# The first expert group's token gather, cut into two halves of 256 columns

## The reference, cut to what matters

```
def moe_ffn(x, router_w, router_bias, w_gate, w_up, w_down):
    aff = sigmoid(x @ router_w)                       # 16 experts, 4 groups of 4
    # the group with the best two-score sum, and its two best experts, per token
    comb = one_hot(e_idx) * gate / sum(gate)          # weight of each token in each expert
    hg = einsum('btd,edf->btef', x, w_gate)           # 2048 -> 512
    hu = einsum('btd,edf->btef', x, w_up)
    h  = silu(hg) * hu * comb[..., None]
    return einsum('btef,efd->btd', h, w_down)         # 512 -> 2048
```

## Time and profile before

| | us |
|---|---|
| median of three runs | 1759.06 |
| the profiled execution's own time | 1759.79 |
| its span in the trace | 1757.9 |
| PE busy | 1596.2 (91%) |
| DVE busy | 720.8 (41%) |
| ACT busy | 467.4 (27%) |

### The profile page before, as it was taken

One profiled execution on the slowest core, in us unless ns is written; L12 is line 12 of the kernel. 1 busy time (PEld: TensorE's weight loads), 2 busy tenths in 40 slices (PEclk: granted clock), 3 DMA queues, 4 the chain that ended last, 5 costly groups with the idle time before them and its releaser, 6 DMA issues.

```text
span 1757.9 us, 18363 instructions
## 1 busy us (share of the span) xinstructions
PE 1596.2 (91%) x7223; PEld 948.4 (54%) x7223; DVE 720.8 (41%) x1220; ACT 467.4 (27%) x693; POOL 16.8 (1%) x36
## 2 busy tenths in 40 slices
PE   8999999998999879898879999999799988989985
PEld 6888887876533224333237888878543323533321
DVE  6675555656211112111157797656521112111116
ACT  4565545432110001000024335553220000100000
POOL 1000000000000000000000000000000000000000
PEclk9999999998999999999999999999899999999998
DMA  8666554784899999999994555538489999999995
GB/s 267 174 180 182 166 158 141 262 310 157 319 416 421 421 416 422 419 422 421 421 361 120 168 167 162 162 121 347 175 354 421 421 421 416 421 415 422 421 419 234
DMA packets 133270, 538.12 MB, mean 306 GB/s; under 512 B 19377, under 2 KB 19505, under 8 KB 86849
## 3 DMA queue, kind: packets, MB, share of 16 engines
q1 hardware_dynamic: 132608, 532.75, 80.0%
q0 software_dynamic: 576, 4.19, 0.6%
HBM read 534.82 MB, written 2.10 MB: 305 GB/s over the span
## 4 chain that ended last, share of the span: by engine, by line
PE 56%; issue 29%; DMA 10%; DVE 3%; ACT 1%; SPq 1%; POOL 0%; POOLq 0%; DVEq 0%; ACTq 0%
PE ps L750 12%; PE ps L752 11%; PE ps L751 11%; PE ps L1035 8%; DMA ring<-in_moe_w_down 5%; PE ps L1097 4%; DMA ring<-in_moe_w_up 4%; PE ps L731 2%; PE ps L1015 1%; PE ps L1016 1%; PE ps L1024 1%; PE ps L1208 1%; PE ps L1222 1%; DMA arena<-in_x 0%; SPq L597 0%
## 5 line engine op out<-in xcount | busy, mean ns | idle before, releaser
L750 PE MATMUL ps<-w_lo,x_hi 128*128 128x512 f32 x880 | 350.7, 399 | 7.5 <-DVE x_lo L2312 2.5
L751 PE MATMUL ps<-w_hi,x_hi 128*128 128x512 f32 x880 | 344.7, 392 | 0.0
L1768 DVE TENSOR_TENSOR w_lo<-ring,w_hi 128x1024 fp32r<-128x1024 f32 x224 | 270.2, 1223 | 181.2 <-ACT w_hi L1315 179.6
L1315 ACT ACTIVATE w_hi<-ring 128x1024 fp32r<-128x1024 f32 x224 | 235.5, 1059 | 311.5 <-PE ps L752 306.8
L2210 DVE TENSOR_TENSOR arena<-ps,arena 128x512 f32<-128x512 f32 x128 | 82.9, 687 | 418.7 <-PE ps L1025 418.7
L750 PEld LDWEIGHTS ps<-w_lo,x_hi 128*128 128x128 f32 x880 | 166.5, 189 | 46.3 <-issue 7.2
L1035 PE MATMUL ps<-arena,hT 128*64 128x512 f32 x768 | 177.1, 616 | 9.6 <-DVE hT L2200 4.3
L751 PEld LDWEIGHTS ps<-w_hi,x_hi 128*128 128x128 f32 x880 | 166.5, 189 | 34.7 <-issue 0.5
L1097 PE MATMUL ps<-ring,arena 128*64 128x512 f32 x768 | 170.5, 594 | 6.4 <-DMA ring<-in_moe_w_down 6.4
L1524 ACT ACTIVATE y_hi<-ps 128x512 fp32r<-128x512 f32 x64 | 36.1, 596 | 459.9 <-PE ps L1097 239.7
L752 PE MATMUL ps<-w_hi,h_lo 128*128 128x512 f32 x384 | 150.2, 391 | 0.0
(11 more groups left out here) (333 smaller groups left out, 1530.8 us busy)
## 6 DMA issues: line engine op xcount, KB each, us to landing
arena<-in_moe_w_gate SPq DMA_DIRECT2D x48, 2048.0 KB, 18.3
ring<-in_moe_w_down SPq DMA_DIRECT2D x96, 1024.0 KB, 18.2
arena<-in_moe_w_up SPq DMA_DIRECT2D x32, 2048.0 KB, 20.4
ring<-in_moe_w_up SPq DMA_DIRECT2D x32, 2048.0 KB, 20.7
ring<-in_ab_w_in SPq DMA_DIRECT2D x96, 512.0 KB, 3.7
ring<-in_moe_w_gate SPq DMA_DIRECT2D x16, 2048.0 KB, 19.9
arena<-in_moe_w_down SPq DMA_DIRECT2D x32, 1024.0 KB, 17.1
ring<-in_c_w_in SPq DMA_DIRECT2D x64, 512.0 KB, 3.7
```

What stands on the lines that cost most here:

```text
L750: nc.tensor.matmul(t, x_h, w_l[:, k, :], start=(opens and k == 0), stop=False)
L751: nc.tensor.matmul(t, x_h, w_h[:, k, :], start=False, stop=False)
L1315: act.activation(high_unit(n), raw_unit(n)[0], ACT.Copy).then_inc(w_hi_ready, 1)
L1768: v.tensor_tensor(lo, raw, high_unit(n).bitcast(FP32), ALU.subtract).then_inc(w_lo_ready, 1)
```

## The change

In the first group, a gather tile is made in two parts. `gather_tile` makes only the first 256 columns (`HALF_GROUP`; the slots of pairs 0 and 1), and the copies are of 256 columns. The other 256 columns (pairs 2 and 3) are made by `gather_rest`: tiles 0 to 7 behind the first pair's last projection step and ahead of the turning of `h_e`, tiles 8 to 15 two by two ahead of each m of the second pair. The first picks are written by halves: the first 256 columns of both blocks where the picks were, the second 256 columns of both behind `low(1,1)`. The first pair's picks are turned (`turn_pick`) behind gather tile 1 instead of ahead of tile 0, and PE starts tile 0 with block 0 alone, without waiting for `pick_ready`. ACT and DVE copy tiles 0 and 1 ahead of `pick_T` and of the gate weights. The second group is unchanged except for the counts that it waits for. The diff, cut to its core (left out: the new semaphore names, and counts that go up by 8):

```diff
+        def rest_at(n):
+            return {4: 13, 5: 14, 6: 16, 7: 17}[n] if n >= 4 else 8 + n
 ...
         def scatter_at(first, i, c):
-            return (8 if first else 10) + 4 * (i - 1) + c
+            if first and i == 1:
+                return {0: 12, 1: 15, 2: 18, 3: 19}[c]
+            return (16 if first else 10) + 4 * (i - 1) + c
 ...
 # PE, gather_tile
-                    if first:
-                        pe.wait_ge(s["h_lo_ready"], TT * (k // 4 + 1))
+                    n = HALF_GROUP if first else BANK
+                    for tt in range(TT):
+                        if first and k == 0:
+                            pe.wait_ge(s["pick_ready"] if tt else s["pick_begun"], 1)
+                        if first and k % 4 == 0:
+                            pe.wait_ge(s["h_lo_ready"], TT * (k // 4) + tt + 1)
+                        nc.tensor.matmul(t[:, 0:n], h_hi[:, tt, mine], pick8[:, tt, 0:n], start=(tt == 0), stop=False)
+                        last = nc.tensor.matmul(t[:, 0:n], h_lo[:, tt, mine], pick8[:, tt, 0:n], start=False, stop=(tt == TT - 1))
+                    last.then_inc(s["full"][b], 1)
+
+                def gather_rest(k):
+                    b = k % 2
+                    pe.wait_ge(s["drained"][b], rest_at(k // 2))
+                    if k == 0:
+                        pe.wait_ge(s["pick_rest"], 1)
+                    t = ps[6 + b][:, 0:BANK - HALF_GROUP]
                     mine = slice(BANK * (k // 4) + k % 4, BANK * (k // 4 + 1), 4)
                     for tt in range(TT):
-                        nc.tensor.matmul(t, h_hi[:, tt, mine], pick8[:, tt, :], start=(tt == 0), stop=False)
-                        last = nc.tensor.matmul(t, h_lo[:, tt, mine], pick8[:, tt, :], start=False, stop=(tt == TT - 1))
+                        nc.tensor.matmul(t, h_hi[:, tt, mine], pick8[:, tt, HALF_GROUP:BANK], start=(tt == 0), stop=False)
+                        last = nc.tensor.matmul(t, h_lo[:, tt, mine], pick8[:, tt, HALF_GROUP:BANK], start=False, stop=(tt == TT - 1))
                     last.then_inc(s["full"][b], 1)
 ...
 # PE, pair
                             for k in range(4 * m, 4 * m + 4):
                                 gather_tile(g, first, k)
+                                if first and k == 1:
+                                    turn_pick()
                             for b in range(2):
                                 pe.wait_ge(s["drained"][b], group_tiles(g) + gather_at(first, 2 * m + 1) + 1)
+                        if first and i == 1:
+                            gather_rest(8 + 2 * m)
+                            gather_rest(9 + 2 * m)
 ...
+                    if first and i == 0:
+                        for k in range(8):
+                            gather_rest(k)
                     pe.wait_ge(s["h_ready"], x + 1)
 ...
-                all_drained(pe, f"xT{lay + 1}" if lay == 0 else f"pos{lay}")
+                all_drained(pe, "xT1" if lay == 0 else None)
 ...
 # ACT, pair (DVE has the odd tiles in the same places, behind h_e)
+                    if not elder:
+                        gathered(g, first, 0)
                     act.wait_ge(s["pT_full"], x + 1)
 ...
                     act.activation(silu_g[:, :], ps[0][:, :], ACT.Silu).then_inc(s["silu_ready"], 1)
+                    if first and i == 0:
+                        for k in range(0, 8, 2):
+                            gathered_rest(k)
                     act.wait_ge(s["hT_full"], x + 1)
 ...
 # DVE
-                pick_half(0, 0)
+                pick_first(0, 0).then_inc(s["pick_begun"], 1)
                 v.wait_ge(psum_full, filled(f"pos{lay}", 1))
                 v.reduce_max(rounds_f[:, 0:1], tile(f"pos{lay}", 1)[:, 0:NE], AX.X).then_inc(drained["D"], 1)
-                pick_half(0, 1).then_inc(s["pick_ready"], 1)
+                pick_first(1, 0).then_inc(s["pick_ready"], 1)
                 low(0, 1)
                 norm(1)
                 for tt in range(TT):
                     low(1, tt)
+                for tt in range(TT):
+                    ins = pick_first(tt, 1)
+                ins.then_inc(s["pick_rest"], 1)
```

More of the change, by code:

```diff
@@ L448, in all_drained @@
             for who in "AD":
-                eng.wait_ge(drained[who], drained_by[:first[stage]].count(who))
+                eng.wait_ge(drained[who], drained_by[:first[stage] if stage else None].count(who))
         w_in = [a["ab_w_in"][0], a["c_w_in"][0]]
@@ L1046, in pair, with turn_pick @@
                     mine = slice(i * P, (i + 1) * P)
+                    def turn_pick():
+                        for tt in range(TT):
+                            nc.tensor.transpose(ps[0][:, tt * P:(tt + 1) * P], pick8[:, tt, mine].bitcast(FP32), ident[:, :])
+                        for tt in range(TT):
+                            last = nc.tensor.matmul(ps[0][:, SEQ:SEQ + 2], pick8[:, tt, mine].bitcast(FP32), comb_g[:, tt, 2 * i:2 * i + 2],
+                                                    start=(tt == 0), stop=(tt == TT - 1), skip_group_check=True)
+                        last.then_inc(s["pT_full"], 1)
                     if not (first and i == 0):
                         pe.wait_ge(s["hT_ready"], x)
[L1049 to L1054, removed]
+                        turn_pick()
                     if i > 0:
@@ L1105, in group @@
                 def group(g, first):
-                    pe.wait_ge(s["pick_ready"], g + 1)
+                    if not first:
+                        pe.wait_ge(s["pick_ready"], g + 1)
                     for i in range(GPAIRS):
@@ L1117, in experts @@
                 for c in (2, 3):
-                    scatter(n_r * PAIRS - 1, 1, c, n_r * 48 - 4 + c)
+                    scatter(n_r * PAIRS - 1, 1, c, n_r * 48 + 4 + c)
                 for b in range(2):
-                    pe.wait_ge(s["drained"][b], n_r * 48)
+                    pe.wait_ge(s["drained"][b], n_r * 48 + 8)
             experts(0)
@@ L1514, in gathered, with gathered_rest @@
                     act.wait_ge(s["full"][0], group_tiles(g) + gather_at(first, k // 2) + 1)
-                    act.activation(xc(k), ps[6][:, :], ACT.Copy).then_inc(s["drained"][0], 1)
+                    n = HALF_GROUP if first else BANK
+                    act.activation(xc(k)[:, 0:n], ps[6][:, 0:n], ACT.Copy).then_inc(s["drained"][0], 1)
+                def gathered_rest(k):
+                    act.wait_ge(s["full"][0], rest_at(k // 2) + 1)
+                    act.activation(xc(k)[:, HALF_GROUP:BANK], ps[6][:, 0:BANK - HALF_GROUP], ACT.Copy).then_inc(s["drained"][0], 1)
                 def rows_hi(x, c, added=None, own=False):
@@ L1538, in pair @@
                     if i == 0:
-                        for k in range(0, 8, 2):
+                        for k in range(0 if elder else 2, 8, 2):
                             gathered(g, first, k)
@@ L1543, in pair @@
                                     high(2 + k // 4, tt)
+                    if first and i == 1:
+                        gathered_rest(8)
                     if i > 0:
                         rows_hi(x - 1, 2, added[0])
+                    if first and i == 1:
+                        gathered_rest(10)
                     if i == 0:
@@ L1550, in pair @@
                         rows_hi(x - 1, 3, added[1])
+                    if first and i == 1:
+                        gathered_rest(12)
+                        gathered_rest(14)
                     act.wait_ge(s["step_used"], STEPS * x + 7)
                     act.activation(silu_g[:, :], ps[0][:, :], ACT.Silu).then_inc(s["silu_ready"], 1)
+                    if first and i == 0:
+                        for k in range(0, 8, 2):
+                            gathered_rest(k)
                     act.wait_ge(s["hT_full"], x + 1)
@@ L2199, in gathered, with gathered_rest @@
                     v.wait_ge(s["full"][1], group_tiles(g) + gather_at(first, k // 2) + 1)
-                    v.tensor_copy(xc(k), ps[7][:, :]).then_inc(s["drained"][1], 1)
+                    n = HALF_GROUP if first else BANK
+                    v.tensor_copy(xc(k)[:, 0:n], ps[7][:, 0:n]).then_inc(s["drained"][1], 1)
+                def gathered_rest(k):
+                    v.wait_ge(s["full"][1], rest_at(k // 2) + 1)
+                    v.tensor_copy(xc(k)[:, HALF_GROUP:BANK], ps[7][:, 0:BANK - HALF_GROUP]).then_inc(s["drained"][1], 1)
                 def rows_lo(x, c):
@@ L2215, in pair @@
                     at = {c: group_tiles(g) + scatter_at(first, i, c) for c in ((2, 3) if i == 0 else range(4))} if elder else None
+                    if not elder:
+                        gathered(g, first, 1)
                     v.wait_ge(s["pT_ready"], x + 1)
@@ L2223, in pair @@
                     if i == 0:
-                        for k in range(1, 8, 2):
+                        for k in range(1 if elder else 3, 8, 2):
                             gathered(g, first, k)
@@ L2233, in pair @@
                         add(0, at[0])
```

(10 more changed lines are left out.)

18 lines of the change are left out of this document (13 added, 5 removed).

## The result

The changed kernel takes 1772.94 us (median of four runs, 1770.03 to 1776.13) against 1759.09 us of the kernel before (four runs by now): 1.0077 times the time before, 95% interval 1.0060 to 1.0094. It is slower by 14 us. The profiled execution is the slowest of the four, 1776.13 us; its gap to the profiled execution before is 16.3 us.

The account below looks back on a forecast made before the run. The DMA's weight stream was taken as the bound, PE setting it only in the first pair. Two layers at 5.8 us more idle plus 1.1 for use 0 gave 12.7 on 1759.79: 1772 us, 80% range 1759 to 1780.

Parts of the forecast that it names:

- A half tile costs as much as a whole one: Gather matmuls of 256 columns still start 0.235 us apart, set by the weight load with its step of four.
- The blocks: First pair, m = 1 to 3: 0.6 us saved a block, DMA holes 5.2 us instead of 6.97, a gain of 1.8.
- the rival of the falling clock: Clock falls in the silu's gap and once in a block, 1.7 us each, both layers: 1778 to 1779 us; 10%.
- The silu's gap: Eight rest tiles ahead of turning `h_e` delay the down steps by 6.7 us, opening a new DMA hole of 6.1 us.
- The second pair: Rest tiles add 2.0 us a block; a DMA hole of 1.35 us, later holes 0.1.
- PE work that lies later is hidden: Behind the second pair PE gains on the DMA and waits, so extra PE work there costs nothing.
- Use 0: Weight issue that PE's step 0 releases: earlier projection against low clock, net +0.25 us in layer 0, +0.85 in layer 1.

Follow-up runs that it names:

- a1: Changed kernel with `h_hi` and `h_lo` reordered so that the gather's weight loads take adjacent columns: 1758.52 us, 0.9988 of the kernel before.
- a3: Changed kernel with its rest tiles one pair later, in the second and third pairs, none in the silu's gap: 1770.84 us, 1.0067 of the kernel before.
- c2: Kernel before, 512-column tiles, picks turned behind tile 1, copies of tiles 0 and 1 ahead of `high(1,.)` and `low(1,.)`: 1760.05 us, 1.0001 of before.
- b2: Kernel before with 20 matmuls of 512 columns added on PE while it waits for the router: 1763.85 us, 1.0023 of before.

## Why the prediction was right, and where it was not

- **A half tile costs as much as a whole one: right.** Starts 0.235 apart, and a1 shows the cause.
- **The blocks: right, but for the clock in one of six.** First gather matmul to projection 444.94 to 449.51, 4.57 us; 4.6 were worked out (3.61 and 0.96, where 3.74 and 0.87 were; the copy's share was written as 0.24 for a difference of 0.22). In layer 1 the loss of the blocks falls by 2.1; 1.8 were forecast. In layer 0 it falls by 0.3 only: the clock was at 0.50 from 449.5 to 453, under the projection of m = 1, and use 2 came 13.28 after use 0 instead of 11.6. That is a piece of the rival of the falling clock, in a block and not in the gap, where the clock stayed at 1.00.
- **The silu's gap: right.** The way from use 7 to use 8 grew by 12.77 - 6.09 = 6.68; 6.7 were forecast. The loss there grew by 5.7 and 6.1 us, 6.1 were forecast.
- **The second pair: right in layer 0's loss, right in layer 1's term.** In layer 0 the way from use 11 to 12 is 10.25, 1.1 longer than before and not 2.0; in layer 1 it is 11.17 for 9.22, 1.95 longer. PE's way to the projection grew in layer 0 as forecast (1.8), but the stretch of low clock (507.8 to 511), which before (500.8 to 504) lay under the projection's start, now lay under the scatter and the rest tiles, and these keep their 0.235 at the low clock. The loss grew by 1.3 and 2.3 where 1.45 was forecast; why layer 1 loses 0.9 more I can't say.
- **"PE work that lies later is hidden": wrong as a rule, and hardly tested by this change,** which adds no gather matmuls behind the second pair. a3 adds 32 there, and the 5 us that it loses at the second group's gather show what becomes of it. I had taken PE's lead at the end of the first group as large without counting it. In the changed kernel the second group loses 1.4 and 0.4 us more than before. In layer 0 that is not shown to be PE's delay: the first down step there ran at the low clock, and took 5.35 us where it takes 3.65, just ahead of the hole. c2, which has no extra matmuls, shows the same fall and loss.

```profile
732.07 5.35 PE L1133 MATMUL ps<-arena 128*64 128x512 f32 x16 [0.86 <-ACT arena L1608]
```
```profile
732.00:736.00 4.00, 3.93 (x12) 0.61 1.02 426
736.00:740.00 4.00, 4.00 (x20) 0.96 0.62 205
```

- **Use 0: right, by two errors that cancel.** +0.18 in layer 0 (+0.25 forecast). In layer 1 it is 8.26 later, of which 7.39 is layer 0's delay (its last routing matmul before the decision, 1249.42 and 1256.81): +0.87 (+0.85 forecast). But the projection started 1.2 us earlier in layer 0 (436.55, where 436.2 was worked out) and 0.7 in layer 1, not 1.5 and 0.9, and at the low clock it lost 1.4 us (8.46 for 7.09) and 1.5, not 1.75.

The sum was 12.7 us; the medians are 13.9 apart, the profiled executions 16.3. What the sum lacks of the profiled difference is the loss in the second group (1.8), the fallen clock in a block of layer 0 (1.5) and the second pair's loss in layer 1 (some 0.9), less some tenths elsewhere. How often the clock falls in the other executions no trace shows, so that the median came within 1 us of 1772 is in part luck.

## What to carry to other kernels

When a matmul's moving operand is made shorter, look at the weight load beside it first: from some width on the load is the pace, and a step in the stationary operand that was nearly free at 512 columns doubles the cost of a tile of 256. Where a stream of transfers is the bound and one stage is not, extra work in that stage is paid at the next place where the transfers have no step in hand; moving it later only helps as far as the slack up to the next such place, which has to be counted. And when a first result is waited for, check what stands ahead of its copy on the copying engines before shortening the matmuls.

## What was not expected of the hardware

- Reading fp32 with a step of four elements costs ACT and DVE too: 631 to 1128 ns and 691 to 1084 ns for 128x512.
- With a step of four in the weight load, matmuls of 256 columns start 0.235 us apart at the full and at the low clock alike (0.235 to 0.24 from 429.98 to 430.92 in the changed kernel). With adjacent columns they start 0.12 apart at the full clock and 0.21 at the low one (a1, at 0.50, below). At the low clock the half tiles therefore do save time even with the step, 0.43 to 0.235.

```profile
431.20 0.41 PE L1027 MATMUL ps<-pick,h_lo 128*128 128x256 f32 x1
431.41 0.41 PE L1026 MATMUL ps<-pick,h_hi 128*128 128x256 f32 x1
```

- In b2 the granted clock came up to 1.00 under 20 dense matmuls and was back at 0.50 ten us later, in the middle of the gather; between, PE had paused 1.34 us ahead of the turning and 1.85 us ahead of tile 2.
